# Filler products at two norm borders, bare state steps, and two weight slots' low parts on VectorE

## The reference, cut to what matters

```python
# first block, after the mixer and after the feed-forward: norm, add, next norm
h = h + rmsnorm(mix, norm_mix_post)
a = rmsnorm(h, norm_ffn_pre) @ w_ffn_in
...
return h + rmsnorm(y, norm_ffn_post)
# second block
h = rms_norm(x, norm_mix[i]);  proj = h @ w_in[i]
attn = windowed_gqa(q, k, v, sink[i])
rw = rwkv7_time_mix(zr, ...)          # a recurrence over 512 tokens, in both directions
merged = gates[..., 0, :] * (attn @ w_up_attn[i]) + gates[..., 1, :] * (rw @ w_up_rwkv[i])
```

## Time and profile before

| | |
|---|---|
| median of three runs | 1821.18 us (1818.89 to 1825.93) |
| profiled execution | 1830.32 us, span 1828.5 us |
| TensorE products / weight loads, busy | 1738.0 us (95%) / 1502.6 us (82%) |
| VectorE, ScalarE, GpSimd, busy | 1023.2 (56%), 653.7 (36%), 110.7 us (6%) |
| mean granted TensorE clock | 0.978 of full speed |

### The profile page before, as it was taken

One profiled execution on the slowest core, in us unless ns is written; L12 is line 12 of the kernel. 1 busy time (PEld: TensorE's weight loads), 2 busy tenths in 40 slices (PEclk: granted clock), 3 DMA queues, 4 the chain that ended last, 5 costly groups with the idle time before them and its releaser, 6 DMA issues.

```text
span 1828.5 us, 38642 instructions
## 1 busy us (share of the span) xinstructions
PE 1738.0 (95%) x17164; PEld 1502.6 (82%) x17164; DVE 1023.2 (56%) x1546; ACT 653.7 (36%) x1073; POOL 110.7 (6%) x125
## 2 busy tenths in 40 slices
PE   7999999799999999899999988887999999999998
PEld 7889888799999999797777767776778888888887
DVE  5256866457636646538654465655585535353555
ACT  4342345434424323443343333333164212121222
POOL 3400000100000000100000000000133000000020
PEclk9999999989999999899999999999799999999999
DMA  6311320302222222312232001000223222222221
GB/s 196 91 57 38 104 70 1 134 30 92 97 96 90 107 94 72 111 70 105 70 110 75 36 4 49 5 4 33 116 81 115 88 97 92 92 92 92 92 92 69
DMA packets 29276, 144.57 MB, mean 79 GB/s; under 512 B 6331, under 2 KB 9675, under 8 KB 14652
## 3 DMA queue, kind: packets, MB, share of 16 engines
q1 hardware_dynamic: 24972, 133.58, 20.5%
q0 software_dynamic: 3856, 7.87, 1.7%
q10 hardware_dynamic: 288, 0.73, 0.1%
HBM read 134.82 MB, written 8.91 MB: 79 GB/s over the span
## 4 chain that ended last, share of the span: by engine, by line
PE 79%; DVE 6%; ACT 3%; issue 3%; POOL 0%; DVEq 0%; ACTq 0%; POOLq 0%
PE g_bank L240 8%; PE g_bank L242 8%; PE g_bank L241 8%; PE f_bank L240 7%; PE f_bank L241 7%; PE f_bank L242 7%; PE r_bank L2543 4%; PE a_bank L1820 3%; PE a_bank L1824 3%; PE a_bank L1822 2%; PE m_bank L667 1%; PE m_bank L795 1%; PE r_bank L2516 1%; PE a_bank L1883 1%; PE m_bank L855 1%
## 5 line engine op out<-in xcount | busy, mean ns | idle before, releaser
L228 DVE TENSOR_TENSOR w_w_lo<-w_w_raw,w_w_hi 128x2048 fp32r<-128x2048 f32 x65 | 148.9, 2291 | 157.5 <-ACT w_w_hi L215 157.1
L240 PE MATMUL f_bank<-u_hi,w_w_hi 128*128 128x258 f32 x704 | 202.4, 287 | 5.4 <-DVE u_lo L1579 4.6
L241 PE MATMUL f_bank<-u_hi,w_w_lo 128*128 128x258 f32 x704 | 201.3, 286 | 0.0
L242 PE MATMUL f_bank<-u_lo,w_w_hi 128*128 128x258 f32 x704 | 199.9, 284 | 0.0
L241 PE MATMUL g_bank<-g_y_hi,g_lo 128*128 128x512 f32 x352 | 139.4, 396 | 0.0
L242 PE MATMUL g_bank<-g_y_lo,g_hi 128*128 128x512 f32 x352 | 139.2, 395 | 0.0
L240 PEld LDWEIGHTS f_bank<-u_hi,w_w_hi 128*128 128x128 f32 x704 | 134.2, 191 | 6.0 <-issue 5.1
L215 ACT ACTIVATE w_w_hi<-w_w_raw 128x2048 fp32r<-128x2048 f32 x65 | 123.9, 1906 | 41.2 <-PE f_bank L242 30.9
L240 PE MATMUL g_bank<-g_y_hi,g_hi 128*128 128x512 f32 x352 | 138.4, 393 | 0.0
L215 ACT ACTIVATE g_hi<-g_raw 128x2048 fp32r<-128x2048 f32 x44 | 84.0, 1908 | 146.3 <-PE g_bank L242 146.3
L242 PEld LDWEIGHTS f_bank<-u_lo,w_w_hi 128*128 128x128 f32 x704 | 135.0, 192 | 0.0
(11 more groups left out here) (545 smaller groups left out, 4044.7 us busy)
## 6 DMA issues: line engine op xcount, KB each, us to landing
g_raw<-in_w_ff SPq DMA_DIRECT2D x32, 1024.0 KB, 4.7
w_w_raw<-in_w_in SPq DMA_DIRECT2D x29, 1024.0 KB, 4.8
w_w_raw<-in_w_ffn_in SPq DMA_DIRECT2D x22, 1024.0 KB, 4.8
w_w_raw<-in_w_ffn_out SPq DMA_DIRECT2D x12, 1024.0 KB, 4.8
w_w_raw<-in_w_o SPq DMA_DIRECT2D x4, 1024.0 KB, 5.1
gate_pre<-rw_t POOLq DMA_DIRECT2D x16, 256.0 KB, 2.3
g_raw<-in_w_up SPq DMA_DIRECT2D x4, 1024.0 KB, 6.0
g_raw<-in_w_out SPq DMA_DIRECT2D x4, 1024.0 KB, 5.0
```

What stands on the lines that cost most here:

```text
L228: nc.vector.tensor_tensor(R.lo[:, r, 0:size], R.raw[:, r, 0:size], R.hi[:, r, 0:size].bitcast(F32), ALU.subtract).then_inc(R.split, 1)
L240: nc.tensor.matmul(out, w_hi, u_hi, start=start, stop=False)
L241: nc.tensor.matmul(out, w_lo, u_hi, start=False, stop=False)
L242: return nc.tensor.matmul(out, w_hi, u_lo, start=False, stop=stop)
```

## The change

- At both norm borders TensorE multiplies the identity by 512 columns of the constants (`keep_warm`), once between the sum of squares and the spread, and four times (FFN) or three times (attention) behind the spread. Each is one float32 product of 128x512 into a PSUM bank that nobody reads.
- The twelve `run_attn(1)` in the state steps are gone. Of the 96 products, 7 still stand among the output products, 53 (not 50) behind them, and 36 (not 27) in the `fi` loop: 0, 8, 6 and 22.
- GpSimd's `low(1)` and `low(2)` are gone. VectorE makes the low part of slot 1 in one instruction after the last state step, and that of slot 2 in two halves, after the gate products of `fi` 0 and `fi` 1.
- ScalarE takes the tiles 0, 1 and 2 out one round later, and tile 5 after the split of group 0 in round `fi` 1, not in round `fi` 0.

```diff
--- before.py
+++ after.py
@@ -298,6 +298,12 @@
     for j in range(groups):
         last = nc.tensor.matmul(out[0:n, j:j + 1], sq[:, n * j:n * j + n], C("ones")[:, 0:1], start=start and j == 0, stop=stop and j == groups - 1)
     return last
+
+
+def keep_warm(nc, C, out, count):
+
+    for _ in range(count):
+        nc.tensor.matmul(out, C("ident"), C.all[:, 0:512], start=True, stop=True)
 
 
 def spread_tokens(pe, nc, C, outs, diag, n, groups):
@@ -1437,8 +1443,10 @@
             sum_tokens(pe, nc, C, bank[:, 4, :], wo_sum, T, TG, True, False)
             pe.wait_ge(wo_squared, KT)
             sum_tokens(pe, nc, C, bank[:, 4, :], wo_sq[:, (KT - 1) % 2, :], T, TG, False, True).then_inc(tok_sum, 1)
+            keep_warm(nc, C, bank[:, 7, :], 1)
             pe.wait_ge(tok_diag, 1)
             spread_tokens(pe, nc, C, [bank[:, 0, :], bank[:, 1, :]], diag, T, TG).then_inc(row_done, 1)
+            keep_warm(nc, C, bank[:, 7, :], 4)
 
             def first_slot(j, q, r):
 
@@ -1769,8 +1777,10 @@
             sum_tokens(pe, nc, C, bank[:, 1, :], ff_sum, P, NB, True, False)
             pe.wait_ge(ff_squared, KT)
             sum_tokens(pe, nc, C, bank[:, 1, :], ff_sq[:, (KT - 1) % 2, :], P, NB, False, True).then_inc(tok_sum, 1)
+            keep_warm(nc, C, bank[:, 3, :], 1)
             pe.wait_ge(tok_diag, 1)
             spread_tokens(pe, nc, C, [bank[:, 0, :]], diag, P, NB).then_inc(row_done, 1)
+            keep_warm(nc, C, bank[:, 3, :], 3)
 
             def qkv_product(k, t, r):
                 w = slice(k * SLOT, k * SLOT + SLOT)
@@ -2451,13 +2461,6 @@
 
         @block.gpsimd
         def _(pool):
-            def low(n):
-                pool.wait_ge(M.R.hi_done, n + 1)
-                nc.gpsimd.tensor_tensor(M.R.lo[:, n % 2, :], M.R.raw[:, n % 2, :], M.R.hi[:, n % 2, :].bitcast(F32), ALU.subtract).then_inc(M.R.split, 1)
-
-            pool.wait_ge(d_done, NU)
-            low(1)
-            low(2)
             for t in range(KT):
                 pool.wait_ge(M.R.tile_free, t + 1)
                 pool.wait_ge(M.gate_open_a, t + 1)
@@ -2694,7 +2697,6 @@
                             last = nc.tensor.matmul(bank[hp(hh), d, fi * HD:fi * HD + HD], gi[hp(hh), c, 4 * d + fi, :],
                                                     s[hp(hh), front, 4 * d + fi, :], start=True, stop=True)
                     last.then_inc(step_done, 1)
-                    run_attn(1)
             pe.wait_ge(state_done, 2 * (NCH - 1))
             pe.wait_ge(rp_read, NU)
             for t in range(NB):
@@ -2713,7 +2715,7 @@
                                                         zr[hp(par), (R_, K_)[d] + fi, tk], s[hp(par), f, 4 * d + fi, :],
                                                         start=(d, f) == dirs[0], stop=(d, f) == dirs[-1])
                 last.then_inc(y_done, 1)
-            run_attn(50)
+            run_attn(53)
             pe.wait_ge(gate_sig, 1)
             pe.wait_ge(gate_loaded, 16)
             pe.wait_ge(yn, NB)
@@ -2727,7 +2729,7 @@
                     last = nc.tensor.transpose(tile(bank[:, 6 + fi % 2, :], t), tile(zr[:, V_ + fi, :], t), C("ident"))
                 last.then_inc(yt, 1)
                 nc.tensor.matmul(bank[:, fi % 2, :], lora_g[:, fi * P:fi * P + P], zr[:, 13, :], start=True, stop=True).then_inc(gl_done, 1)
-                run_attn((0, 6, 3, 18)[fi])
+                run_attn((0, 8, 6, 22)[fi])
 
         @block.scalar
         def _(act):
@@ -2841,14 +2843,13 @@
                 late(u)
             act.wait_ge(rp_read, NU)
             hi_slot(act, nc, M.R, 0, 1, None)
-            keep_attn(0)
             for t in range(NB):
                 act.wait_ge(centred, t + 1)
                 if t >= 2:
                     act.wait_ge(var, t - 1)
                 nc.scalar.activation(tiles(bz[:, t % 2, :]), zr[:, V_:V_ + RW_FI, t * P:t * P + P], ACT.Square).then_inc(ysq, 1)
-                if t in (1, 2):
-                    keep_attn(t)
+                if t:
+                    keep_attn(t - 1)
             act.wait_ge(var, NB)
             nc.scalar.activation(stat[:, 1], stat[:, 1], ACT.Sqrt, scale=1.0 / HD, bias=GN_EPS).then_inc(gstd, 1)
             keep_attn(3)
@@ -2860,10 +2861,10 @@
                     act.wait_ge(rw_done, fi - 1)
                 nc.scalar.activation(bz[:, fi % 2, :], bank[:, 6 + fi % 2, :], ACT.Identity, scale=column("lnx_w", fi),
                                      bias=column("lnx_b", fi)).then_inc(scaled, 1)
-                if fi == 0:
+                if fi:
+                    split_branch(fi - 1)
+                if fi == 1:
                     keep_attn(5)
-                else:
-                    split_branch(fi - 1)
                 open_gate(fi)
             split_branch(RW_FI - 1)
             for t in (6, 7):
@@ -2972,6 +2973,13 @@
                     last = nc.vector.tensor_tensor(M.R.lo[:, 0, c], M.R.raw[:, 0, c], M.R.hi[:, 0, c].bitcast(F32), ALU.subtract)
                     if n == 7:
                         last.then_inc(M.R.split, 1)
+
+            def third_low(part):
+                dve.wait_ge(M.R.hi_done, 3)
+                c = slice(1024 * part, 1024 * part + 1024)
+                last = nc.vector.tensor_tensor(M.R.lo[:, 0, c], M.R.raw[:, 0, c], M.R.hi[:, 0, c].bitcast(F32), ALU.subtract)
+                if part == 1:
+                    last.then_inc(M.R.split, 1)
 
             def branch_low(fi):
                 dve.wait_ge(M.rw_split_hi, fi + 1)
@@ -3058,6 +3066,7 @@
                         nc.vector.tensor_tensor(at, bank[:, d, 0:256].rearrange("p (a b) -> p a b", a=4), at, ALU.add).then_inc(step_add, 1)
                         dve.wait_ge(step_add, 2 * (step - 1) + d + 1)
                     nc.vector.tensor_tensor(at, at, pc[:, c, us].unsqueeze(2).broadcast_to([P, 4, HD]), ALU.mult).then_inc(state_done, 1)
+            lo_slot(dve, nc, M.R, 0, 1)
             y = lambda t: zr[:, V_:V_ + RW_FI, t * P:t * P + P].rearrange("p a (b c) -> p a b c", b=2)
             per_head = lambda k, t: stat[:, k, t, :].rearrange("p (a b) -> p a b", a=4)
             over_head = lambda k, t: per_head(k, t).unsqueeze(3).broadcast_to([P, 4, 2, HD])
@@ -3086,6 +3095,8 @@
                 dve.wait_ge(with_bonus, fi + 1)
                 dve.wait_ge(gl_done, fi + 1)
                 nc.vector.tensor_tensor(rw_t[:, fi, :], bank[:, fi % 2, :], bz[:, fi % 2, :], ALU.mult).then_inc(rw_done, 1)
+                if fi < 2:
+                    third_low(fi)
                 if fi:
                     branch_low(fi - 1)
             branch_low(RW_FI - 1)
```

## The result

| | before | after |
|---|---|---|
| median, executions run side by side | 1821.83 us (4) | 1809.08 us (4; 1805.15 to 1809.85) |
| side by side again, on another occasion | 1821.82 us (16) | 1806.41 us (6; 1804.03 to 1809.28) |
| ratio, first and second time | | 0.9913 (0.9885 to 0.994), 0.9913 (0.9896 to 0.9931) |
| all executions of this study | 1821.6 us (90; 1812.2 to 1830.6) | 1807.6 us (10; 1804.0 to 1809.9) |
| profiled execution, span | 1830.32, 1828.5 us | 1805.15, 1803.4 us |

The change is faster, by some 14 us in the medians of all executions; forecast were 20.7 less than the median, 1800, with a range of 1795 to 1812. The two profiled executions stand 25 apart, far more than the medians. That difference between what two traces say and what the medians say is the subject of most of the experiments.

A forecast was written before the change was run, and what follows sets the result against it. TensorE was taken to lose time to the low clock at two norm borders and in the state steps, held by attention products. 5.5 + 7.5 + 6.0 + 2.7 - 0.6 - 0.4 = 20.7 off the median 1821.2 gave 1800, range 1795 to 1812.

The forecast's parts named there:

- The borders: Both norm borders: products on constants keep or raise the clock for the groups behind them, 13.0 us gained.
- 5.5: Border to the FFN: with the clock still up, eight groups end at 384.5 instead of 390.0, 5.5 us gained.
- 7.5: Border to attention: groups at 2.29 each bring the sum of group six to 779.05 from 786.57, 7.5 us gained.
- Late products: Both borders: at the low clock the constants' products would not fit their waits, together 5.1 us too long.
- the clock falls at the borders all the same: Rival at both borders: the 13.0 is lost, less up to 5.1 more; 1813 to 1819 us, chance 0.15.
- State steps: State steps: nine periods fall from 1.77 to 1.10 (6.0) and the long scaling shortens (2.7), together 8.7 us.
- the upper bound: State steps: about 11 us gained if the clock rises and VectorE's two operations of 0.42 set the period.
- What VectorE gets: Slot 1's low part (2.3) hidden, 0.4 to spare; slot 2's halves in the `fi` loop: 2.6 gone, 2.3 come.
- The scalings: Behind the output products: scalings come 0.6 us later, a copy now standing between last square and root; term -0.6.
- The `fi` loop: `fi` loop: nine more attention products add 1.9 of work, partly filling a wait of 1.50; term -0.4 us.
- The steps keep their period: Rival in the state steps: TensorE's own sequence sets 1.77, so 6.0 is lost; 1806.5 us, chance 0.13.
- The low clock outlasts the steps: Rival in output products and `fi` loop: clock stays low through the rest, +16 us; 1837 us, chance 0.05.

The follow-up runs named there:

- e10: The kernel before, unchanged, a third trace: 1821.3 us (one execution).
- e5: The changed kernel, unchanged, run again: 1806.4 us, ratio 0.9913 against the kernel before.
- e8: The changed kernel with four attention products moved from the last group to ahead of the first state step: 1808.4 us, ratio 0.9916 against the kernel before.
- e6: The changed kernel without the nine products on constants at the borders: 1811.7 us, ratio 0.9935 against the kernel before.
- e3: The kernel before with only the state steps freed of attention products and the copies out of PSUM one round later: 1815.0 us, ratio 0.997.
- e1: The kernel before, unchanged, run again with a second trace: 1821.3 us, ratio 1.0005.
- e4: The kernel before with only the low parts of slots 1 and 2 moved from GpSimd to VectorE: 1820.8 us, ratio 0.9987.
- e9: The same kernel as e4 (only the low parts moved to VectorE), run once more: 1817.1 us, ratio 0.9976 against the kernel before.
- e12: The changed kernel with two instead of four products behind the FFN spread and four attention products ahead of the steps: 1807.4 us, ratio 0.9923 against before.
- e7: The changed kernel with the nine products on constants cut from 512 to 64 columns: 1810.5 us, ratio 0.9943 against the kernel before.
- e2: The kernel before with only the nine products on constants at the norm borders: 1817.6 us, ratio 0.998.
- e11: The changed kernel with the attention products back in the state steps, old counts and copy order: 1814.0 us, ratio 0.9967 against the kernel before.

## Why the prediction came out as it did

The direction was right, the time lay inside the range, and the forecast of 20.7 was some 6 to 7 too large in the medians of all executions (14), 5 by the ratios (0.0087 x 1821.8 = 15.8; 12.6 to 18.9 by the narrower interval).

**The borders, 13.0 forecast, 4.0 to 4.2 measured.** This is the term that failed. Its step was to price the low stretches by the one profiled execution, and the earlier trace rows, and then to take the sum off the median. Against that execution the working was good: 5.5 was 5.2, 7.5 was 6.5, and the products were hidden but for 0.7 at the attention border (first group 9.6 behind the last FFN product, before 8.9). So was its reason for taking the whole 13.0, that a few wide products in a row raise the clock even where it falls: that is what the attention border does. But the text itself set that execution 9.1 above the median and gave no reason for the 9.1. The reason is this term: in an execution at the median (e10) the same two borders stand 4.1 and 3.6 shorter, and 7.7 of the 13.0 weren't there to be gained. A sum made against an outlier may be taken off the median only after asking which of its terms are what made it one.

**Late products, forecast up to 5.1 if the clock falls.** It came with 1.1 and 1.2 at the FFN border, in e5 and e8; at the attention border the first group is at most 0.2 later than in e10. The rival "the clock falls at the borders all the same" is thus half true: it falls in nearly every trace, for less long and mostly where it costs nothing.

**State steps, 8.7 forecast, about 10.6 measured.** Of the 12.2 between the two traces, 1.6 is a stall ("issue") that stood inside the first step of before and stands ahead of the steps after ([2.33 <-issue]); nothing is gained by that. The periods gave 8.1 instead of 6.0, since the clock rose inside the steps: 0.835, not 1.10, for the second half; the upper bound had this. It is counted from the third addition, which stands at 1269.64 after and, in VectorE's rows of before, here:

```profile
1286.15 0.42 DVE L3058 TENSOR_TENSOR r_s<-r_bank,r_s 128x256 f32<-128x256 f32 x1 [0.42 <-PE r_bank L2694]
```

From there to the output products it is 1303.06 - 1286.15 = 16.9 before and 1278.45 - 1269.64 = 8.8 after. The rest of the 10.6, 2.5, lies where the long scaling stood. By the executions, bare steps and low parts together bring 10.1 (e6).

**What VectorE gets.** Slot 1's low part was forecast as hidden with 0.4 to spare. It isn't quite: with the clock up, the output products come sooner, and VectorE reads the first 1280.52 - 1278.45 = 2.07 behind their start, against 1286.62 - 1285.02 = 1.60 in e3 without the low part; 0.5 is on the path. The scalings are later by this and by the copy ahead of the root: from the output products to the first transpose 21.45, against 1312.93 - 1292.45 = 20.48 in e1, 1.0 where 0.6 was forecast. The two causes can be told apart: e3 (copies moved, no low part) has 20.99, e4 (low part, old order of copies) 20.96. The comparison is with e1 because its output products run at the full level, as after; where they begin at the low one, in the profiled execution and in e10, the same way is 21.5 and nothing was lost.

**The `fi` loop, -0.4 forecast, +0.9 measured.** From the first transpose to the merge block 1313.46 - 1299.90 = 13.6, against 14.4 in e1. TensorE has no wait in it where e1 had 1.51 and 1.05. The nine more products fill those waits instead of coming on top, and the merge block starts as the last of them ends. Neither part does this alone, which the forecast's separate prices could not show: 14.8 in e3, with the products moved and GpSimd's low part kept, 14.4 in e4 and e9, with the reverse, and 13.6 in e6 with both. GpSimd's gate products do block VectorE there, as the prediction let stand; GpSimd and VectorE, after:

```profile
1303.44 1.64 POOL L2467 TENSOR_TENSOR g_branch_a<-g_branch_a,g_gate_a 128x512 f32<-128x512 f32 x1 [273.21 <-ACT g_gate_a L2810]
```

```profile
1303.99 1.64 DVE L3094 TENSOR_TENSOR acc<-acc,rw_t 128x512 f32<-128x512 f32 x1
```

The addition takes 1.64 where its kind takes 0.7, beside a gate product that ends at 1305.08, and TensorE's row of products covers it. The Trainium skill's rule ("SBUF — State Buffer", the shared port pair) agrees here as it does in e3.

**The rivals.** "The steps keep their period" is refuted by 1.05 and 0.835. "The low clock outlasts the steps" is refuted too: 1.00 from 1271.5 on. The error is in the size of the borders, 9 too large, and is partly undone by steps and loop, which gave 2 to 3 more than forecast: 4.1 + 10.6 - 1.0 + 0.9 = 14.6, beside the 14 of the medians. That the errors have opposite signs is luck.

## What to carry to other kernels

Where the clock falls in short gaps, the loss is a property of an execution as much as of the kernel: take several traces before a stage is priced, and compare the profiled execution's own time with the median first. The chain of narrow state steps ran at the low level for a part of its length or all of it in every trace here but one (e12), and what is put between such steps costs at that level: move wide products out of a chain that goes on at the low clock. Filling a gap paid here only with wide products, and only with so many as fit it at the low level too. And price two changes that share a wait together: the `fi` loop gained only with both.

## What the runs showed of the chip that was not expected

- Executions of one kernel on one core differ by 18 us (1812.2 to 1830.6), and the same falls of the clock differ in place and length between them. Between its profiled execution and e10, 9.0 apart, the two borders make up 7.7. Steps of 22.3 and 17.5 in two traces of one other kernel (e9, e4) are a third such place; that it is what takes executions of before down to 1812 is not shown, since its three traces have 23.8 to 24.3.
- Wide products in a gap shortened a fall of the clock more often than they prevented it: 3.4 us at 0.50 instead of 13.7 at the attention border, in all six traces with them. With products of 64 columns TensorE was busy 4.09 of 5.00 us in e7 and stayed at 0.50.
- With attention products between the state steps the clock stayed low for 17 to 27 us in six traces of seven, TensorE busy 5.00 of 5.00; without them, for 10 us or less in seven of seven.
- A stall of TensorE with no releaser ("issue") moves with the program: 1.1 to 2.2 inside the first step in each trace without the nine products (before, e1, e3, e4, e6, e9, e10), and 0.6 to 2.6 ahead of the steps in each of the seven that have them (after, e2, e5, e7, e8, e11, e12). In e7 they are thin, so it goes with their number and not with their width. That it is the loading of instructions is only argued; no run here tested it.
